# A fused two-layer diffusion step on one NeuronCore: expert results weighted and gated as they leave PSUM, instead of after they are gathered

## What is computed

```python
g_w, g_idx = top_k(softmax(x @ w_group + b_group), 1)          # one of 4 groups
e_val, e_idx = top_k(logits of the 4 experts in that group, 2)
e_w = softmax(e_val) * g_w                                     # two weights per token
hid = silu(x @ w_gate[e]) * (x @ w_up[e])
out = sum over the two chosen experts of e_w[e] * (hid @ w_down[e])
xp = xp + gate_prompt * out      # for the 128 prompt tokens
xs = xs + gate_latent * out      # for the 512 latent tokens
```

## Time and profile before

| | |
|---|---|
| median of 3 runs | 1293.53 us (1292.93 to 1294.64) |
| span of the profiled execution | 1292.1 us |
| PE busy | 1231.2 us (95%) |
| DVE busy | 582.2 us (45%) |
| ACT busy | 414.0 us (32%) |
| POOL busy | 57.9 us (4%) |

### The profile page before, as it was taken

How to read it: one execution, slowest core, us unless ns; L and a number is a source line. 1 busy time by engine, 2 the same in 40 slices (tenths; PEclk the granted TensorE clock), 3 DMA queues, 4 the chain that set the end, 5 groups by cost and what they waited for, 6 DMA issues and landing times.

```text
span 1292.1 us, 17212 instructions
## 1 busy us (share of the span) xinstructions
PE 1231.2 (95%) x5561; PEld 681.7 (53%) x5562; DVE 582.2 (45%) x1310; ACT 414.0 (32%) x859; POOL 57.9 (4%) x63
## 2 busy tenths in 40 slices
PE   7999999999999999998978998899999999999997
PEld 4554566666664475443435444466654574444442
DVE  1322555555552574322217444888834663222215
ACT  2432444444451120111113326677722111111122
POOL 0103000000000020000011000000000110000002
PEclk9999999999999999999999999999999999999998
DMA  9979999622253067999976001500020369989946
GB/s 373 413 310 407 415 412 411 256 100 99 99 204 147 33 231 241 353 356 358 368 281 266 9 1 36 229 2 1 1 98 2 123 259 347 351 268 352 358 169 242
DMA packets 88357, 290.18 MB, mean 225 GB/s; under 512 B 9209, under 2 KB 27580, under 8 KB 86876
## 3 DMA queue, kind: packets, MB, share of 16 engines
q1 hardware_dynamic: 46032, 185.68, 39.1%
q0 software_dynamic: 16640, 64.59, 12.7%
q10 hardware_dynamic: 25612, 38.96, 8.9%
HBM read 214.48 MB, written 74.73 MB: 224 GB/s over the span
## 4 chain that ended last, share of the span: by engine, by line
PE 81%; DMA 4%; DVE 4%; ACT 3%; SPq 3%; issue 2%; ACTq 1%; DVEq 0%; POOL 0%; POOLq 0%
PE ps L2099 16%; PE ps L1709 11%; PE ps L1726 11%; PE ps L2128 8%; PE ps L1651 7%; PE ps L1979 6%; PE ps L1942 4%; PE ps L1754 3%; PE ps L1803 3%; PE ps L2178 3%; PE ps L1671 2%; DMA arena<-in_moe_gu 2%; PE ps L1935 2%; PE ps L1952 2%; PE ps L2041 2%
## 5 line engine op out<-in xcount | busy, mean ns | idle before, releaser
L2099 PE MATMUL ps<-arena 128*128 (+1 forms) x560 | 247.9, 596 | 0.0
L2099 PEld LDWEIGHTS ps<-arena 128*128 128x128 f32 x560 | 104.4, 191 | 118.4 <-issue 118.3
L1651 PE MATMUL ps<-const,arena 128*128 128x128 f32 (+2 forms) x1000 | 144.0, 277 | 18.3 <-DMA const<-in_const 8.4
L1709 PE MATMUL ps<-arena 128*128 128x512 f32 (+2 forms) x400 | 152.1, 535 | 5.0 <-DVE arena L1111 1.8
L1651 PEld LDWEIGHTS ps<-const,arena 128*128 128x128 f32 (+2 forms) x1000 | 114.7, 141 | 76.9 <-issue 39.6
L1149 DVE TENSOR_REDUCE hst<-ps 128x1 f32<-128x640 f32 (+1 forms) x160 | 110.8, 713 | 94.3 <-PE ps L1979 80.1
L1726 PE MATMUL ps<-arena 128*128 128x512 f32 x320 | 142.0, 596 | 1.4 <-issue 1.4
L2128 PE MATMUL ps<-arena 128*128 (+1 forms) x280 | 126.1, 593 | 2.2 <-ACT arena L850 2.2
L727 ACT ACTIVATE arena<-ps,hst 128x640 f32<-128x640 f32 (+1 forms) x160 | 112.4, 706 | 42.0 <-DVE hst L1149 42.0
L1709 PEld LDWEIGHTS ps<-arena 128*128 128x128 f32 x400 | 74.4, 190 | 74.4 <-issue 58.3
L1726 PEld LDWEIGHTS ps<-arena 128*128 128x128 f32 x320 | 59.1, 190 | 69.8 <-issue 69.7
(11 more groups left out here) (213 smaller groups left out, 1212.2 us busy)
## 6 DMA issues: line engine op xcount, KB each, us to landing
arena<-in_moe_gu SPq DMA_DIRECT2D x128, 512.0 KB, 12.7
arena<-in_ada_w SPq DMA_DIRECT2D x62, 768.0 KB, 11.8
slot_rows<-arena POOLq DMA_DIRECT2D x10, 4096.0 KB, 68.1
arena<-in_moe_w_down SPq DMA_DIRECT2D x64, 512.0 KB, 15.8
slot_rows<-arena ACTq DMA_DIRECT2D x33, 512.0 KB, 8.7
arena<-slot_rows ACTq DMA_DIRECT2D x124, 128.0 KB, 13.1
arena<-mod_rows SPq DMA_DIRECT2D x12, 512.0 KB, 12.6
arena<-in_gqa_w_qkv SPq DMA_DIRECT2D x12, 512.0 KB, 14.8
```

The source lines that it names most:

```text
L1651: return nc.tensor.transpose(out, in_, ident[0:rows, 0:rows])
L1709: last = mm(bank(2 + b, cols), hT[l](t)[:, k * P:(k + 1) * P], w[:, k], start=k == 0, stop=k == KD - 1)
L2099: last = mm(bank(gu_bank(u)), e_xsT[:, nth(u, D)][:, k * P:(k + 1) * P], w(k * BANK, BANK), start=k == 0, stop=k == KD - 1)
```

## The change

The two weights per token move into a tile `shares`, beside a mark that is 1 for the prompt tile and 0 elsewhere, and are computed before the first copies and the plan (`weights`, called right behind the last `choose_first`). The same function waits for the gate rows and replaces the prompt's gate row by its difference to the latents'. POOL scatters `shares` to a second DRAM table `slot_shares` of 8 bytes per slot row, in ten more indirect transfers per layer. ACT loads the 128 pairs of a slot tile behind its rows, on the same semaphore `xs_landed` (`load_share`, 1 KB to 128 partitions); those of tiles 0 to 3 stand behind the rows of tile 3, and behind a wait for the scatters. `xsT` and the new `gate_of` wait for them.

The result leaves PSUM through DVE (`y_gated`): multiplied by the row's weight and by the gate row that `gate_of` has put together for this tile (difference times mark, plus the latents' gate). ACT only stores it. After the gathers, layer 0 only adds, and in layer 1 PE takes the gathered rows as they are. `combine_first`, `gate_chosen`, `chosen` and `scale` go.

```diff
@@ -443,6 +448,10 @@
             dst = split(e_xs[q * XB:(q + 1) * XB, nth(u, D)], P // XB)
             src = slots[ds(row, P), q * (D // XQ):(q + 1) * (D // XQ)].rearrange("(r b) c -> b r c", b=XB)
             eng.dma_start(dst, src).then_inc(S(f"xs_landed{u % RING_N}", l), 16)
+
+    def load_share(eng, l, row, u, dst):
+
+        eng.dma_start(dst[:, 2 * (u % RING_N):2 * (u % RING_N) + 2], slot_shares[ds(row, P), :]).then_inc(S(f"xs_landed{u % RING_N}", l), 16)
 
     def rounds_needed(eng, l):
 
...
@@ -635,7 +645,14 @@
                     pool.indirect_dma_start(
                         slots, bass.IndirectOffsetOnAxis(ap=slot_i[:, 2 * t + c:2 * t + c + 1], axis=0),
                         e_h[:, t * D:(t + 1) * D], None).then_inc(S("rows_scattered"), 16)
+            pool.wait_ge(S("weighted"), l + 1)
+            for t in range(NTILE):
+                for c in range(2):
+                    pool.indirect_dma_start(
+                        slot_shares, bass.IndirectOffsetOnAxis(ap=slot_i[:, 2 * t + c:2 * t + c + 1], axis=0),
+                        shares[:, 4 * t + 2 * c:4 * t + 2 * c + 2], None).then_inc(S("shares_scattered"), 16)
             pool.wait_ge(S("rows_scattered"), 32 * NTILE * l + 16 * 2 * NTILE)
+            pool.wait_ge(S("shares_scattered"), 32 * NTILE * (l + 1))
 
             wait_landed(pool, ("gu", l, FED))
             pool.nop().then_inc(S("gu_ready"), 1)
...
@@ -840,26 +848,20 @@
                 row = act.value_load(first_row[0:1, ds(t, 1)], min_val=0, max_val=SPARE_ROW)
                 act.wait_ge(S("xsT_ready", l), t - (RING_N - 1))
                 load_rows(act, l, row, u)
-
-            def y_out(t, u, r, last=False):
+                load_share(act, l, row, u, share_in)
+
+            def y_out(t, u, last=False):
                 row = act.value_load(first_row[0:1, ds(t, 1)], min_val=0, max_val=SPARE_ROW)
-                act.wait_ge(S("y_done", l), t + 1)
-
-                act.wait_ge(S(f"y_stored{u % RING_N}", l), r * 16 + 16)
                 y = e_y[:, nth(u, D)]
-                act.activation(y, ps[:, 6 * BANK:8 * BANK], ACT.Copy).then_inc(S("y_out", l), 1)
                 act.wait_ge(S("y_out", l), t + 2)
                 stored = S("last_stored") if last else S(f"y_stored{u % RING_N}", l)
                 act.dma_start(slots[ds(row, P), :], y).then_inc(stored, 16)
 
 
-            def last_y_out(t, u, r):
+            def last_y_out(t, u):
                 row = act.value_load(first_row[0:1, ds(t, 1)], min_val=0, max_val=SPARE_ROW)
-                act.wait_ge(S(f"y_stored{u % RING_N}", l), r * 16 + 16)
                 y = e_y[:, nth(u, D)]
-                for n, done in enumerate((S("half_y"), S("y_done", l))):
-                    act.wait_ge(done, t + 1 if n else l + 1)
-                    act.activation(y[:, n * BANK:(n + 1) * BANK], bank(6 + n), ACT.Copy).then_inc(S("y_out", l), 1)
+                for n in range(2):
                     act.wait_ge(S("y_out", l), t + 2 + n)
                     act.dma_start(slots[ds(row, P), n * BANK:(n + 1) * BANK], y[:, n * BANK:(n + 1) * BANK]).then_inc(S("last_stored"), 16)
 
@@ -876,21 +878,26 @@
             R = rounds_needed(act, l)
             row = act.value_load(first_row[0:1, RING_N:RING_N + 1], min_val=0, max_val=SPARE_ROW)
             load_rows(act, l, row, RING_N)
+            act.wait_ge(S("shares_scattered"), 32 * NTILE * (l + 1))
+            for x in range(FED):
+                load_share(act, l, x * CAP, x, share)
+            load_share(act, l, FED * CAP, FED, share_in)
+            load_share(act, l, row, RING_N, share_in)
             with act.Fori(0, ROUNDS) as i:
                 with act.If(i < R):
                     for u in range(RING_N):
                         rows_of(i * RING_N + (u + 4), u + 4)
                         sil(i * RING_N + (u + 1), u + 1)
-                        y_out(i * RING_N + u, u, i)
+                        y_out(i * RING_N + u, u)
             for k in range(SLOT_TILES - LOOPED):
                 if k + 1 < SLOT_TILES - LOOPED:
                     sil(R * RING_N + (k + 1), k + 1)
                 else:
                     act.activation(table_of[:], ones[:, 0:1], ACT.Sqrt)
                 if k + 1 < SLOT_TILES - LOOPED:
-                    y_out(R * RING_N + k, k, R + k // RING_N, k >= SLOT_TILES - LOOPED - RING_N)
+                    y_out(R * RING_N + k, k, k >= SLOT_TILES - LOOPED - RING_N)
                 else:
-                    last_y_out(R * RING_N + k, k, R + k // RING_N)
+                    last_y_out(R * RING_N + k, k)
 
         r_sh, r_ex = e_r[:, R_SH:R_SH + NTILE * (NG + 1)], e_r[:, R_EX:R_EX + NTILE * (NG + 1)]
 
@@ -956,13 +963,9 @@
             square(t, e_junk)
 
         square_g(0)
-        scale(0, 1)
         late_columns(1)
-        scale(0, 2)
         square_g(1)
-        scale(0, 3)
         square_g(2)
-        scale(0, 4)
         square_g(3)
 
 
...
@@ -1481,14 +1487,19 @@
             nc.vector.tensor_copy(split(stage[:, 0:4 * TT], 4)[:, :, 0:FIXED], split(const[:, C_T2 + 4 * FIXED * l:C_T2 + 4 * FIXED * (l + 1)], 4))
             op(nc.vector.tensor_reduce(s_rounds, need, AX.X, ALU.add))
             nc.vector.tensor_copy(plan[:], stage).then_inc(S("routed"), 1)
-
-            ex = rt(R_EX, T5 * (NG + 1))
+            settle()
+
+        def weights(l):
+
+            T5 = NTILE
+            den, ex = rt(T_LG, T5), rt(R_EX, T5 * (NG + 1))
             dve.wait_ge(S("r_exp"), l + 1)
             op(nc.vector.tensor_reduce(den, split(ex[:, 0:T5 * NG], T5), AX.X, ALU.add))
             op(nc.vector.scalar_tensor_tensor(den, ex[:, T5 * NG:], 1.0, den, ALU.add, ALU.mult))
-            op(nc.vector.reciprocal(w_pair[:, 0:T5], den))
-            op(nc.vector.tensor_tensor(w_pair[:, T5:], w_pair[:, 0:T5], ex[:, T5 * NG:], ALU.mult)).then_inc(S("weighted"), 1)
-            settle()
+            op(nc.vector.reciprocal(w_first, den))
+            op(nc.vector.tensor_tensor(w_second, w_first, ex[:, T5 * NG:], ALU.mult)).then_inc(S("weighted"), 1)
+            dve.wait_ge(S("gates_m"), 32 * (l + 1))
+            op(nc.vector.tensor_tensor(gate_m[:, 0:D], gate_m[:, 0:D], gate_m[:, D:2 * D], ALU.subtract))
 
         def experts(l):
 
@@ -1533,13 +1544,15 @@
             choose_first(NTILE - 2)
             place_rows(l, NTILE - 1)
             choose_first(NTILE - 1)
+            weights(l)
 
             def xsT(t, u, r=0):
-                dve.wait_ge(S(f"xs_landed{u % RING_N}", l), r * 16 * XQ + 16 * XQ)
+                dve.wait_ge(S(f"xs_landed{u % RING_N}", l), r * LANDED + LANDED + (0 if u == FED or u == FED + RING_N else 16))
                 if not isinstance(t, int):
 
                     dve.wait_ge(S("gu_done", l), t - 1)
-                c = nth(u, D)
+                c, k = nth(u, D), 2 * (u % RING_N)
+                nc.vector.tensor_copy(share[:, k:k + 2], share_in[:, k:k + 2])
                 nc.vector.transpose(e_xsT[:, c].rearrange("p (k r b) -> p k r b", k=KD, b=XB),
                                     e_xs[:, c].rearrange("p (r a k) -> p k r a", k=KD, a=XB)).then_inc(S("xsT_ready", l), 1)
 
@@ -1547,6 +1560,23 @@
                 dve.wait_ge(S("sil_ready", l), t + 1)
                 c = nth(u, FF)
                 nc.vector.tensor_tensor(e_hid[:, c], bank(gu_bank(u), FF, FF), e_sil[:, c], ALU.mult).then_inc(S("hid_ready", l), 1)
+
+            def gate_of(u):
+
+                if u < FED:
+                    dve.wait_ge(S(f"xs_landed{u}", l), LANDED + 16)
+                k = 2 * (u % RING_N)
+                nc.vector.scalar_tensor_tensor(e_gate, gate_m[:, 0:D], share[:, k + 1:k + 2], gate_m[:, D:2 * D], ALU.mult, ALU.add)
+                settle()
+
+            def y_gated(t, u, r, first=0, end=2):
+
+                k, b = 2 * (u % RING_N), slice(first * BANK, end * BANK)
+                dve.wait_ge(S(f"y_stored{u % RING_N}", l), r * 16 + 16)
+                dve.wait_ge(*(S("y_done", l), t + 1) if end == 2 else (S("half_y"), l + 1))
+                nc.vector.scalar_tensor_tensor(e_y[:, nth(u, D)][:, b], ps[:, 6 * BANK:8 * BANK][:, b], share[:, k:k + 1], e_gate[:, b],
+                                               ALU.mult, ALU.mult).then_inc(S("y_out", l), 1)
+                settle()
 
             def hidT(t, u):
                 dve.wait_ge(S("hid_turned", l), t + 1)
@@ -1565,6 +1595,8 @@
                         hidT(i * RING_N + u, u)
                         xsT(i * RING_N + (u + 2), u + 2, i)
                         hid(i * RING_N + (u + 1), u + 1)
+                        gate_of(u)
+                        y_gated(i * RING_N + u, u, i)
             for k in range(SLOT_TILES - LOOPED):
                 if l == 0 and k == 1:
                     modulation(1, 1)
@@ -1573,43 +1605,20 @@
                     xsT(R * RING_N + (k + 2), k + 2, R)
                 if k + 1 < SLOT_TILES - LOOPED:
                     hid(R * RING_N + (k + 1), k + 1)
-        def gate_row(t):
```

(48 more changed lines are left out.)

29 lines of the change are left out of this document (14 added, 15 removed).

## The result

The changed kernel takes 1329.88 us (median of 4 runs, 1327.05 to 1331.15), the kernel before 1293.93 us (4 runs on the same chip, 1292.93 to 1294.64): a ratio of 1.0275, 95% interval 1.0260 to 1.0289. It is 36 us slower. The profiled execution has a span of 1326.9 us and took 1328.73 us.

The account below looks back on a forecast made before the run. PE was taken as the bound, 95% busy, with layer 0's loop nearly transfer-bound. Terms 19.8 - 0.3 + 17.6 - 0.6 = +36.5 us on a 1292.1 us span gave 1328.6, carried to a 1330 us median; forecast case 1316 to 1338, range 1305 to 1343.

Parts of the forecast that it names:

- The two waits: At each expert stage's start: gate rows, +4.3 and +1.4 us; share of tile 2 before turn 1, +14.2 and +14.4 us.
- The turn of a small load: In ACT's queue, each share load waits behind one of SP's weight pieces: 1.7 us each, 5.1 us for three.
- the smaller sum: By the skill's fixed 2 us, three overlapping share loads end 2 us behind the rows, not 5.1; sum about 6 us smaller.
- The rival with cheap small transfers: Share loads cost no turn and land with or just behind the rows: 1322 us, chance 0.17.
- that in which the queue does not hold the order: Rival: shares pass the rows in ACT's queue, so only their issues count: 1306 us, chance 0.10.
- The rival with dear small packets: In the full loop each share costs what rows do, first turns 2.2 us or more: 1340 to 1346 us, chance 0.13.
- the faster one: Rival: scatters and loads get through early, leaving only the gain at the ends: down to 1291 us, chance 0.04.
- So 5.4 remain: Layer 0's loop: weight waits of 7.6 us, less 5.5 for a smaller backlog, plus 3.3 for share packets; -2.2 us.
- The 3.3 us for the packets of the added loads: In layer 0's loop, share loads add 0.33 us per tile over 10 tiles to the weight waits.
- The ends: Ends of the expert stages: products removed after the gathers, less DVE's longer chain before the last down; -0.3 and -0.6 us.
- I put nothing on it: Early in the expert stage, gate_of of tiles 0 and 1 waits for rows and shares of tiles 3 and 4: 0 us.
- Scatters "covered": POOL's ten scatters per layer, about 1.3 us each, end before ACT's wait for them matters: no cost.

Follow-up runs that it names:

- e2: Changed kernel, but the wait for the gate rows and their subtraction stand behind the plan instead of ahead of the first copies: 1320.89 us.
- e4: Changed kernel with two more 1 KB loads between the shares of tiles 1 and 2, to columns nobody reads: 1334.93 us.
- e1: Changed kernel, but ACT waits for the scatters and loads the shares of tiles 0 to 2 ahead of the plan: 1315.47 us.
- e8: Kernel before the change with gathered rows only added; the products by weight and gate left out, so the output lacks them: 1293.85 us.
- e3: Changed kernel with the edits of e1 and e2 together: 1317.46 us.
- e5: Changed kernel, gates waited for behind the plan; POOL loads the first three shares, ACT later ones behind write-backs; the transpose waits for rows alone: 1302.64 us.
- e7: Kernel before the change with one idle load of 128 x 8 bytes per tile behind the rows, which the transpose waits for: 1298.28 us.
- e9: Kernel before the change with the ten extra scatters per layer alone, which POOL waits for and nobody reads: 1297.34 us.
- e10: e5 without scatters and loads of shares; weight and mark are ones, so its output lacks the weights: 1296.47 us.
- e6: e5, but each layer's last tile but one leaves PSUM by a scaling copy on ACT, and DVE multiplies by the gate later: 1302.60 us.

## Why the prediction was right, and where not

The two waits and their size were foreseen; that the total, 1330 us against 1329.88, is so close is luck, since errors of its terms cancel. In us of the profiled execution:

| step | predicted | measured |
|---|---|---|
| ahead of the experts of layer 0 | 0 | +2.0 |
| gates' wait, layer 0 | +4.3 | +4.8 |
| clock behind it | +1.7 | +1.6 |
| wait for the share of tile 2, layer 0 | +14.2 | +12.1 |
| clock behind it | +1.8 | +2.6 |
| given back in the weight-bound tiles | -2.2 | -7.4 |
| between the layers, up to the projection | -0.3 | +1.3 |
| from there to the feed of layer 1 | 0 | +0.4 |
| gates' wait, layer 1 | +1.4 | +2.1 |
| wait for the share of tile 2, layer 1 | +14.4 | +13.1 |
| clock behind it | +1.8 | +1.4 |
| end | -0.6 | +0.8 |
| sum | +36.5 | +34.8 |

**The two waits** were right in place and releaser, and in size within 2.1 us. e2 shows the wait for the share by itself at 14.0 and 15.0 us, and without the gates' wait the median falls by 9.0 us. The turn of a small load, taken at 1.7 us, measured 1.3 in the changed kernel and 1.4 to 2.1 in e4. The Trainium skill ("DMA: Bandwidth & Descriptors", "Anatomy of one DMA — SWDGE (gpsimd) path") gives a fixed part of about 2 us, nearly all completion, fitted on transfers that GpSimd issues. In e1, with no weights in line, the three loads on ScalarE's queue land 1.7 to 1.9 us after their issue and overlap, which is near it. Behind rows and weights they land one after another, each adding a turn, so there the measurement decides against the smaller sum. The rival with cheap small transfers falls with e4, that in which the queue does not hold the order falls with the landings. The rival with dear small packets falls with the time and with the changed kernel's tiles, none of which waits for weights in either layer; the faster one falls with e8, which has the whole gain of the ends and none of the waits.

**"So 5.4 remain", of 7.6 us of weight waits,** is the step that failed most: none remained. PE stood for 12.83 us ahead of turn 1, and with that start nothing was late any more; 5.5 us, from one load's landing on an empty queue, was too small a measure of that lead. In e2, e3 and e4, with pauses of 4.67 to 15.70 us, the delay also shrinks by 6.0 to 7.5 us between turns 2 and 15. In e1 it shrinks by 2.8 and in e5, where PE hardly stands, it grows by 2.5; there PE doesn't wait for weights either, but for `hid`. The 3.3 us for the packets of the added loads are close to the 2.7 of e7 by luck: they were meant as lateness of the weights, and in e7 they are ACT's issues and the Silu behind them.

**The ends** had the wrong sign: -0.9 us predicted, +2.1 measured, and +3.1 without the 1.0 us behind the last store. The cost, DVE's chain ahead of the last `down`, was seen, at 0.7 us in each layer; it is 1.2 in layer 0 and 0.8 in layer 1. "Gain 1.0 us" and "about 1.3 us after the landing earlier" took the products away and did not ask what comes right behind them; e8 shows it, the weights of the third block and the next gather.

**"I put nothing on it"**, of `gate_of` waiting for tiles 3 and 4, held in the changed kernel alone. e1 shows some 4 us in each layer once the cover is gone.

**The range.** The bounds that the sum lists, all taken at once, reach from 1311 to 1336 us, not from 1316 to 1338; the measured time lies within both.

**Scatters "covered"**: so in the changed kernel. Alone they cost 1.5 us in the profile (e9), and in e3 their length decides when the shares are issued.

**Ahead of the experts**, 2.0 us of that execution belong to no step of the change.

## What to carry to other kernels

Folding a factor into an earlier step moves its deadline: gates and shares that had been wanted at the end of the expert stage were wanted at its start, behind transfers that nobody had needed to hurry. Give a small operand its own semaphore and let only the operation that uses it wait; in front of a transpose that feeds PE, 8 bytes per row cost 12 to 15 us in each layer, and with the shares kept apart the whole change costs 8 in all. Look at what an engine's own order holds behind its issues of transfers: where the DMA engines were full, the issues of four pieces took up to 6.8 us instead of 1.8, and here a Silu stood behind them. Before work is taken off an engine at a wait, look at what lands next: here removing all of it gained nothing that could be measured.

## What the runs showed of the hardware

An execution can lose 2 to 3 us near 105 us, in a stage that no edit touches. The window from 100 to 120 us, of the kernel before and of the changed one (columns as in the earlier trace rows):

```profile
100.00:120.00 20.00, 18.01 (x80) 8.73 (x79) 4.46 (x11) 8.37 (x22) 10.15 (x12) 1.00 1.02 402
```
```profile
100.00:120.00 20.00, 18.00 (x78) 8.93 (x76) 4.46 (x11) 8.58 (x22) 10.69 (x13) 0.91 1.01 398
```

PE is equally busy, 18.0 us, and has in it the same two pauses of 0.8 and 1.2 us, but the granted clock is 1.00 in one and 0.91 in the other. The profiles of e1 to e3, e5, e7, e8 and e10 show 1.00 and reach the feed of layer 0 within 0.3 us of the kernel before, that of e4, with 1.00 too, 0.6 us later; those of the changed kernel, e6 and e9 show 0.91 and are 2.0, 3.0 and 1.9 us later there. The 12 runs of e8 fall apart in the same way, six from 1292.5 to 1293.3 us and six from 1294.5 to 1295.9. So 1 or 2 us between two medians, as of e6, or part of e9's, can come from how often this happens. What decides it stays open.

The price of a small load was new, too: 1.3 to 2.1 us for 1 KB behind the 512 KB pieces of another queue, and 1.7 to 1.9 us from issue to landing, three of them overlapping, where no such pieces were in line (e1). And an issue is not always short: in the full stretch of layer 0 the four row pieces of a tile took ACT 1.8 us before the change and 4.4 to 6.8 us in e7, with one small load more per tile.
